# Norms by token parts: latent columns of all features first, the last squares summed by PE, and squares over the outputs between two layers

## What is computed

```python
def rmsnorm(x, g):
    xf = x.astype(jnp.float32)
    y = xf * lax.rsqrt(jnp.mean(xf * xf, axis=-1, keepdims=True) + EPS)
    return (y * g.astype(jnp.float32)).astype(x.dtype)

x = x + gt2 * conv_ffn(modulate(rmsnorm(x, norm2_g[layer]), sh2, sc2), ...)   # first two layers
...
hx = rmsnorm_2(x, g_pre) * (1 + scale[:, None]) + shift[:, None]              # last two layers
x_new = x + gate[:, None] * rmsnorm_2(y, g_post)
```

## Time and profile before

| | |
|---|---|
| runs, median | 2902.92 us (2902.10, 2902.92, 2913.47) |
| profiled execution, own time | 2902.85 us |
| its span | 2901.0 us |
| mean granted clock of PE | 0.946 of full speed |
| PE busy, its instructions | 2635.5 us (91%), 14496 |
| DVE, ACT, POOL busy | 1297.1, 932.1, 173.3 us |
| chain that ended last, by engine | PE 82%, DVE 10%, ACT 4%, DMA 2% |

### The profile page before, as it was taken

The page is one execution under the profiler, slowest core; times in us unless marked ns, Lnnn a source line. Parts: engine busy times, 40 slices in busy tenths (PEclk is TensorE's granted clock), DMA queues, the critical chain, the costliest instruction groups (busy, mean ns, idle before and its releaser), DMA issues.

```text
span 2901.0 us, 35381 instructions
## 1 busy us (share of the span) xinstructions
PE 2635.5 (91%) x14496; PEld 2032.7 (70%) x14496; DVE 1297.1 (45%) x2324; ACT 932.1 (32%) x1619; POOL 173.3 (6%) x134
## 2 busy tenths in 40 slices
PE   4988799997999999989998989999979989949997
PEld 2765555585888888867876667777858866828765
DVE  3235378835333333354435453334452264373463
ACT  3234355623212122234233332222332143332342
POOL 0000001001101011010000010101100001000010
PEclk9999889997999999998999899999979999969898
DMA  5123300011343332211120135553211210102201
GB/s 213 64 70 92 119 13 1 1 44 59 114 132 110 123 118 68 68 55 59 59 73 1 30 121 169 167 171 127 88 55 62 60 54 1 54 23 84 98 1 58
DMA packets 66001, 223.20 MB, mean 77 GB/s; under 512 B 7216, under 2 KB 10928, under 8 KB 65072
## 3 DMA queue, kind: packets, MB, share of 16 engines
q1 hardware_dynamic: 63648, 214.13, 22.9%
q10 hardware_dynamic: 2192, 6.82, 0.6%
HBM read 218.82 MB, written 2.10 MB: 76 GB/s over the span
## 4 chain that ended last, share of the span: by engine, by line
PE 82%; DVE 10%; ACT 4%; DMA 2%; issue 1%; POOL 0%; SPq 0%; DVEq 0%; ACTq 0%
PE pair L959 21%; PE pair L961 20%; PE pair L960 20%; PE pair L1069 4%; DVE T L1790 3%; PE side L934 2%; PE side L1133 2%; PE pair L982 2%; ACT T L1448 2%; PE pair L1120 1%; DMA RAW<-in_w 1%; PE pair L1002 1%; DVE HL L1782 1%; PE pair L653 1%; PE pair L652 1%
## 5 line engine op out<-in xcount | busy, mean ns | idle before, releaser
L959 PE MATMUL pair<-HH,WH 128*128 128x512 f32 (+1 forms) x2432 | 886.5, 365 | 70.2 <-DVE HL L1782 67.5
L961 PE MATMUL pair<-HH,WL 128*128 128x512 f32 (+1 forms) x2432 | 865.6, 356 | 0.0
L960 PE MATMUL pair<-HL,WH 128*128 128x512 f32 (+1 forms) x2432 | 865.3, 356 | 0.0
L959 PEld LDWEIGHTS pair<-HH,WH 128*128 128x128 f32 x2432 | 465.3, 191 | 192.8 <-DVE HL L1782 87.9
L1558 DVE TENSOR_TENSOR WL<-RAW,WH 128x1024 fp32r<-128x1024 f32 (+4 forms) x286 | 320.7, 1121 | 513.0 <-ACT WH L1224 500.4
L961 PEld LDWEIGHTS pair<-HH,WL 128*128 128x128 f32 x2432 | 466.6, 192 | 65.8
L960 PEld LDWEIGHTS pair<-HL,WH 128*128 128x128 f32 x2432 | 467.3, 192 | 62.1 <-issue 2.6
L1224 ACT CAST WH<-RAW 128x1024 fp32r<-128x1024 f32 (+4 forms) x286 | 270.3, 945 | 548.9 <-DMA RAW<-in_w 531.6
L959 PE MATMUL pair<-DH,WH 128*128 128x512 f32 (+3 forms) x624 | 232.8, 373 | 8.4 <-POOL DL L1977 4.3
L960 PE MATMUL pair<-DL,WH 128*128 128x512 f32 (+3 forms) x624 | 223.6, 358 | 0.0
L961 PE MATMUL pair<-DH,WL 128*128 128x512 f32 (+3 forms) x624 | 223.1, 358 | 0.0
(11 more groups left out here) (278 smaller groups left out, 2754.1 us busy)
## 6 DMA issues: line engine op xcount, KB each, us to landing
RAW<-in_w SPq DMA_DIRECT2D x345, 512.0 KB, 3.6
RAW<-in_w SPq DMA_DIRECT2D x49, 384.0 KB, 3.1
RAW<-in_w SPq DMA_DIRECT2D x16, 256.0 KB, 2.7
DFL<-in_dft_lat ACTq DMA_DIRECT2D x4, 1024.0 KB, 7.7
X<-in_x SPq DMA_DIRECT2D x1, 3072.0 KB, 16.4
out_x<-X SPq DMA_DIRECT2D x8, 256.0 KB, 2.0
RAW<-in_w SPq DMA_DIRECT2D x12, 128.0 KB, 2.0
RAW<-in_w SPq DMA_DIRECT2D x8, 144.0 KB, 2.1
```

The source lines that it names most:

```text
L959: mm(out[0:j.m, c:e], wh[k], a, start=k == 0, stop=False)
L960: mm(out[0:j.m, c:e], wh[k], b, start=False, stop=False)
L961: ins = mm(out[0:j.m, c:e], wl[k], a, start=False, stop=k == j.k - 1)
```

## The change

A new `lat_first(t0)` gives the latent range first, then the context. In all six norms and both posts the sums, Ln and Exp, and in the norms the scaling, shift and splitting, are done for the latents of all eight k and then for the context of all eight. The last feature's square is not added by DVE: PE adds T[2] and T[1] with two matmuls that accumulate. Behind a norm with t0 = 0 whose first two jobs also have t0 = 0 (a1, a2, b1, s0), PE computes the latents of both jobs in two pieces of 256 columns and then the context of both. In `yout` the square comes before the copy to YB. Between the two last layers the squares of the new X go to YB, over the outputs that are used up, and PE adds all eight k by itself; of the context DVE adds four k before norm s1's latents and four behind them, and PE sums its squares before the third job. Many waits of an engine on itself are left out. The modulation of `post` moves from AB to PAB. `pe_wait_rhs` waits for the part that a piece needs.

```diff
+def lat_first(t0):
+    return [(0, 0, LAT)] if t0 else [(0, CTX, TOK), (1, 0, CTX)]
...
 # PE
-            for c in range(0, n, 512):
-                e = min(n, c + 512)
+            for c, e in tokens or [(c, min(n, c + 512)) for c in range(0, n, 512)]:
...
+                    elif key[2] == (a < CTX) or (key[2] == 0 and b > CTX):
+                        pe.wait_ge(*step(*key, k))
...
+        def sums_of(s, first, last, key):
+            mm(sum_psum(s), ONES, first, start=True, stop=False)
+            mm(sum_psum(s), ONES, last, start=False, stop=True).then_inc(*pe.mark(*key))
+        def sums_of_columns(s, a, b):
+            for k in range(KD):
+                pe.wait_ge(*step("nsq", "s1", s, k))
+                ins = mm(sum_psum(s), ONES, YB[:, k, a:b], start=k == 0, stop=k == KD - 1)
+            ins.then_inc(*pe.mark("nss", "s1", s))
...
+                held = [j for j in js if j.kind != "ada"][0:2]
+                normed = state["first"] and not any(j.t0 for j in held)
...
+                    if stage == 0 and normed and j is held[0]:
+                        job(j, [(512, TOK), (CTX, 512)], last=False)
+                    elif stage == 0 and normed and j is held[1]:
+                        job(j, [(512, TOK), (CTX, 512)], last=False)
+                        for x in held:
+                            job(x, [(0, CTX)])
+                    elif stage == 0:
+                        if state["columns"] and j not in held:
+                            sums_of_columns(1, 0, CTX)
+                            state["columns"] = False
...
             elif p[0] == "norm":
-                sums(T[2], ONES, n, P, ("nss", q["id"]), ("nacc", q["id"]))
+                if q["id"] == "s1":
+                    sums_of_columns(0, CTX, TOK)
+                    state["columns"] = True
+                else:
+                    pe.wait_ge(*step("nacc", q["id"], KD - 2))
+                    for s, a, b in lat_first(q["t0"]):
+                        pe.wait_ge(*step("nsq", q["id"], s, KD - 1))
+                        sums_of(s, T[2][:, a:b], T[1][:, a:b], ("nss", q["id"], s))
...
 # ACT, yout
-                act.wait_ge(*act.own())
-                A(YB[:, i, 0:n], ps, AF.Copy, scale=1.0).then_inc(*act.mark())
...
-                A(T[i % 2][:, 0:n], ps, AF.Square).then_inc(*act.mark("psum_read", j.n))
+                A(T[i % 2][:, 0:n], ps, AF.Square).then_inc(*act.mark("ysq", j.layer, i))
+                A(YB[:, i, 0:n], ps, AF.Copy, scale=1.0).then_inc(*act.mark("psum_read", j.n))
...
 # ACT, norm
+                if not late:
+                    act.wait_ge(*step("xready", q["id"]))
+                    for s, a, b in lat_first(t0):
+                        root(s, a, b)
+                for s, a, b in lat_first(t0):
+                    if late:
+                        if s:
+                            squares_of_columns(s, a, b)
+                        root(s, a, b)
+                    for k in range(KD):
+                        t = (T[0], T[1], T[4], T[5])[k % 4]
+                        act.wait_ge(*step("nmul", q["id"], s, k))
                         dst = t[:, a:b] if k in POOL_LO else HH[:, k, t0 + a:t0 + b]
-                        act.wait_ge(*act.own())
                         A(dst, t[:, a:b], AF.Identity, bias=modv(q["blk"], q["shift"] + k, s)).then_inc(*act.mark())
...
 # DVE
+        def add_post(l, k, s, a, b):
+            STT(YB[:, k, a:b], YB[:, k, a:b], PAB[:, s, k:k + 1], T[3][:, a:b], ALU.mult, ALU.mult).then_inc(*dve.mark())
+            dve.wait_ge(*dve.own())
+            TT(x, x, YB[:, k, a:b], ALU.add).then_inc(*dve.mark("xfin", l, s, k))
...
+                for s, a, b in lat_first(t0):
+                    if q["id"] == "s1" and s:
+                        for k in range(4, KD):
+                            add_post(0, k, s, a, b)
+                    dve.wait_ge(*step("nrstd", q["id"], s))
+                    for k in range(KD):
...
+                        STT(t[:, a:b], X[:, k, t0 + a:t0 + b], AB[:, s, k:k + 1], T[3][:, a:b], ALU.mult, ALU.mult).then_inc(*dve.mark("nmul", q["id"], s, k))
+                        if k >= 2:
+                            lo(s, a, b, k - 2)
...
 # DVE, post
+                for s, a, b in lat_first(t0):
+                    dve.wait_ge(*step("prstd", l, s))
+                    for k in range(4 if s else KD):
+                        add_post(l, k, s, a, b)
```

More of the change, by code:

```diff
@@ L64, in __init__ @@
         self.sq = None
+        self.pair = None
 def stream(jobs):
@@ L915, in _ @@
         mm = nc.tensor.matmul
-        state = {"hready": [], "first": True}
+        state = {"hready": [], "first": False, "columns": False}
         def take(bank):
@@ L920, in take, with job @@
                 pe.wait_ge(*step(*key))
-        def job(j):
+        def job(j, tokens=None, last=True):
             s = j.n % NRING
@@ L938, in job @@
                 return
-            pr = uses[0] % 2
-            uses[0] += 1
-            take(pr)
-            pe.wait_ge(*step("lo", j.n))
+            if j.pair is None:
+                j.pair = uses[0] % 2
+                uses[0] += 1
+                take(j.pair)
+                pe.wait_ge(*step("lo", j.n))
+            pr = j.pair
             out = pairs[pr]
@@ L1201, in _ @@
                 l = p[1]
-                n = TOK if l == 0 else LAT
-                sums(T[2], ONES, n, P, ("pss", l), ("pacc", l))
-                free[2] = [("prstd", l, "ln")]
+                t0 = 0 if l == 0 else CTX
+                take(2)
+                pe.wait_ge(*step("pacc", l, KD - 2))
+                pe.wait_ge(*step("psq", l))
+                for s, a, b in lat_first(t0):
+                    sums_of(s, T[2][:, a:b], T[1][:, a:b], ("pss", l, s))
+                free[2] = [("prstd", l, s, "ln") for s, a, b in lat_first(t0)]
     @block.scalar
@@ L1345, in square, with squares_of_columns @@
                 act.wait_ge(*step("nacc", q["id"], k - 2))
-            act.wait_ge(*act.own())
-            A(T[k % 2 if k else 2][:, 0:n], X[:, k, q["t0"]:TOK], AF.Square).then_inc(*act.mark("nsq", q["id"], k))
+            if k < KD - 1:
+                if col:
+                    act.wait_ge(*step("xcol", col.n))
+                A(T[k % 2 if k else 2][:, 0:n], X[:, k, q["t0"]:TOK], AF.Square).then_inc(*act.mark("nsq", q["id"], k))
+                return
+            for s, a, b in lat_first(q["t0"]):
+                if col and not (s and col.t0):
+                    act.wait_ge(*step("xcol", col.n, s))
+                A(T[1][:, a:b], X[:, k, q["t0"] + a:q["t0"] + b], AF.Square).then_inc(*act.mark("nsq", q["id"], s, k))
+        def squares_of_columns(s, a, b):
+            for k in range(KD):
+                act.wait_ge(*step("xfin", 0, s, k))
+                A(YB[:, k, a:b], X[:, k, a:b], AF.Square).then_inc(*act.mark("nsq", "s1", s, k))
         def mlsilu(i):
@@ L1362, in _ @@
             act.also("act_end", pi)
-            if p[0] in ("norm", "lownorm", "attn", "mlstm", "post"):
+            if p[0] in ("norm", "lownorm", "attn", "mlstm", "post") and (p[0] != "norm" or p[1]["id"] != "s1"):
                 act.wait_ge(*step("dve_end", pi))
@@ L1387, in _ @@
                             act.wait_ge(ctx_reloaded, 16)
-                        square(q, k)
+                        square(q, k, j if j.kind == "addx" else None)
                     if stage == 1:
@@ L1604, in epilogue @@
                 dve.wait_ge(*step("mm", j.n))
-                for s, a, b in segs(j.t0):
+                for s, a, b in lat_first(j.t0):
                     x = X[:, m["col"], j.t0 + a:j.t0 + b]
-                    dve.wait_ge(*dve.own())
-                    STT(x, pairs[pr][:, a:b], modv(m["blk"], m["gate"] + m["col"], s), x, ALU.mult, ALU.add).then_inc(*dve.mark())
+                    STT(x, pairs[pr][:, a:b], modv(m["blk"], m["gate"] + m["col"], s), x, ALU.mult, ALU.add).then_inc(*dve.mark("xcol", j.n, s))
                 dve.also("psum_read", j.n)
```

131 lines of the change are left out of this document (57 added, 74 removed).

## The result

The changed kernel took 2875.31 us (median of 6 runs, 2871.65 to 2884.08), the kernel before beside it 2901.80 (2891.37 to 2913.47): a ratio of 0.9905, 95% interval 0.9885 to 0.9925. So it is faster by 0.95%, as forecast: 2875 against 2870, inside the range of 2860 to 2884. The profiled execution took 2875.46 (before: 2902.85), 27.4 less.

The account below looks back on a forecast made before the run. DVE's chain of squares, scaling and splitting was taken to bound the norms and post steps, PE everything else. Gains of 4.7+0.8+5.7+1.4+5.7+13+1.3 = 32.6 us from 2902.85 gave 2870, range 2860 to 2884.

Parts of the forecast that it names:

- T0 to the third job: Halved norms, from DVE's start of scaling (T0) to the third job: T0+29.6 against T0+34.7, 5.1 us gained.
- about 4 us: Held jobs after the last latent low half: PE at the low clock at first, 16 pieces at 0.21 us.
- the sign of being wrong: Held jobs of the halved norms: pieces of 0.21 us beyond the first 20 would show the forecast wrong.
- The start of the norm: Ahead of T0: PE's second matmul replaces DVE's last add; net 0.6 us earlier in b1, s0, a2, 0.4 later in a1.
- a2: Norm a2: val 0's late split and gate 1's late load eat nearly all the gain; 0.8 us gained, gate 1 at T0+36.5.
- 27.3, and twice 24 context pieces, 33.1: Norm a2: after val 0's weights at 21.5, 48 pieces end at T0+27.3 and the context pieces at T0+33.1.
- b2: Norm b2, without halves: loses the last add (0.8) and own waits (0.5), gets a second sum; 1.4 us gained.
- I take the high level: Norm b2: two sums at the high clock take 1.97 us; at the low level 0.4 us is lost.
- Between the last layers: Post step and s1: scaling starts 17.5 us earlier, PE idles 9, low clock costs 2.1; 13 us gained.
- The end: Last post phase: copy and add leave the way of the sums, STT overlap; 1.3 us gained.
- rival 1: Norms a1, a2, b1, s0: clock stays low through both held jobs, costing 34 us, time 2904; chance 0.08.
- rival 5: Norms: POOL's subtractions wait for a running DVE instruction, some 1 us a norm, 5 in all, time 2875; chance 0.05.

Follow-up runs that it names:

- run 1: Changed kernel with PE again taking the two held jobs of a1, a2, b1 and s0 in the old order, columns 0 to 511 first: 2886.07 us, ratio 0.9929.
- run 6: Changed kernel with the waits of DVE, ACT and POOL on themselves put back in the norms: 2876.92 us in one run.
- run 9: Changed kernel with the last square of a1, a2, b1, b2 and s0 added by DVE again and one set of ones-matmuls: 2870.23 us in one run.
- run 2: Changed kernel with the first side job of the modulation after val 0 in the first feed-forward stage: 2873.46 us, ratio 0.9889.
- run 5: Changed kernel with no low halves given to POOL, DVE doing all eight of a half: 2859.88 us, ratio 0.9856.
- run 4: Changed kernel with PE's eight context sums in s1 ahead of the second held job: 2873.77 us, ratio 0.9886.
- run 7: Changed kernel with s1's context half behind the splits and epilogues that jobs 3 and 4 need: 2866.52 us, ratio 0.9870.
- run 11: Changed kernel with a2's side jobs after gate 1, plus the edits of run 3, run 7 and run 5: 2840.55 us, ratio 0.9770.
- run 12: Kernel before the change, with no low halves given to POOL and nothing else: 2900.03 us, ratio 0.9981.
- run 3: Changed kernel with b2's last square added by DVE again and one ones-matmul of 512 columns: 2879.53 us in one run.

## Why the prediction was right, and where it was not

- **T0 to the third job** (29.6 forecast; 29.3, 29.7, 29.8 measured) is right, and by its mechanism: run 1 takes PE's order away and gets 33.5 and 34.2. Within it two sizes were off and hardly mattered: the latent half 12.8 to 13.0 for 12.7, the context half 7.7 for 7.1 (its own terms, 6.5 and 0.3, make 6.8). The own waits gave 0.3 to 0.5 in these latent halves, where 0.5 was taken (run 6). The "about 4 us" at the low level stood on no row; it was 3.2, 4.3 and 4.7 us behind the last latent low half in a1, b1 and s0, which makes 14, 19 and 21 pieces of 0.21 (the sign of being wrong was more than 20). In other profiles it was down to 1.5.
- **The start of the norm**: the sum was about right (T0 came 1.0, 1.8 and 0.9 earlier in a2, b1 and s0, for 0.6), but its working put the gain in the wrong term. "PE adds it with a second matmul", 1.03 earlier, gives nothing on the whole; Ln and Exp of the latents alone, ahead of the context, give 1.3 (run 9). In a1 T0 came 0.4 later, as forecast; with one sum it would have come 1.3 earlier.
- **a2**: forecast 0.8 gained, measured 1.3 lost, and 1.6 more in gate 1 at the low level. The mechanism (late split, late load) was named and runs 1 and 2 show it; the failed step is "27.3, and twice 24 context pieces, 33.1" with gate 0's end at 30.2. The held pieces were counted at the high level from the start. PE restarted at 682.32 (T0+22.7, forecast 21.5, which took the context half as done at 19.2, where it took until 20.8), 12 pieces came at 0.21, gate 0 ended at T0+32.8, and the load and split behind it moved by as much.
- **b2**: "I take the high level" failed. The sums ran low after 2.67 us idle, and 0.7 was lost, where the bound of that step said 0.4. Of the runs with two sums there, only run 5's (6.5 us to T0) had the high level throughout.
- **Between the last layers**: DVE's scaling started 17.4 us earlier relative to the last output matmul (forecast 17.5), PE was idle 10.7 (forecast 9), job 3 lost 2.4 to the low clock (2.1). The chain is right in every step, and runs 4 and 7 take it apart; but it gave 11.1 us net, not 13. The context half took 7.7 us, not 6.7, and the written sum is short: 2575.0+3.7+1.0+6.7+1.05+1.23 is 2588.7, not 2588.0.
- **The end**: 1.3, as forecast.
- **The rivals**: rival 1 (clock low through the held jobs) falls: from 2125.4 on, 12.3 us before the third job of s0, the pieces came every 0.12 us. Rival 5 was the strongest of what I held unlikely, and its mechanism is there: POOL and DVE hold each other both ways. The row that I put against it was no evidence. DVE's low half ahead of the subtraction of the earlier trace rows had only 0.14 us left; in run 6, norm b1, 0.66 us were left:

```profile
1694.24 0.75 DVE L1782 SCALAR_TENSOR_TENSOR HL<-T,MOD,HH 128x512 fp32r<-128x512 f32 x1
...
1299.89 0.75 DVE L1855 SCALAR_TENSOR_TENSOR HL<-T,MOD,HH 128x512 fp32r<-128x512 f32 x1
1299.98 1.80 POOL L2014 TENSOR_TENSOR HL<-T,HH 128x512 fp32r<-128x512 f32 x1 [0.74 <-ACT HH L1491]
```

The subtraction of 512 columns took 1.28 us with 0.14 left, 1.75 with 0.63 left (s0, changed kernel) and 1.80 with 0.66 left: what is left of DVE's instruction and 1.12 to 1.14 more each time, and 1.27 to 1.29 where nothing was left. The 1.28 by itself can't tell the two apart, but the subtractions of 768 columns in the kernel before took 2.08 us with 0.40 left and 2.13 with 0.45. So POOL did wait for DVE. The Trainium skill ("SBUF — State Buffer", "SBUF: two separate sides") says of the port pair that the two engines share that it is held for a whole instruction by the one which starts first; these rows agree. But rival 5's price, 1 us a norm on the latent half, didn't come: the latent half was 12.8 us in b1 and s0, where POOL's first subtraction waited 0.63 us, and 13.0 in a1, a2 and b2, where none did. That the time was rival 5's 2875 is chance. What I had missed is the other direction, POOL holding DVE, in work which the change left in place: run 5 prices it at 8 to 11 us in the stages.

The total was right partly by balance. The stages gave 29.2 up to the third jobs, of which the low clock took 4.0 back in s1 and a2: 25.2, where 32.6 were forecast. The start of the program gave 2.8 by chance, and the rest lost 0.6. The POOL hold as the cause of these 8 to 11 us is shown by one constant, twice (runs 5 and 11), and by the groups of DVE; that it was neutral in the kernel before is measured (run 12), and the account of why is worked out from its rows, not tested by itself.

## What to carry to other kernels

When a chain of one engine holds up PE, order PE's own pieces by what arrives first, and check each place for what sits behind in program order on the other engines: three stops of PE in the changed kernel (4.6 and 2.6 us in a2, 10.7 in s1) were weights split or loaded late because of where that stood in an order, not because of its length. Ask of an offload to POOL what DVE's instructions take with and without it. A mean of 1087 ns against 752 for one form is the hint, and the sum over all forms decides: the same offload cost 5.0 us of DVE's time in the changed kernel and 2.4 in the kernel before, where removing it gave nothing clear of the noise. Judge a change of a few us by stage lengths between fixed landmarks, since one stretch at the low clock moves the total by 6, and take more than one profile where the clock level within the stage differs.

## What the hardware showed that I had not expected

- POOL's 512-column subtraction took 1.27 to 1.29 us where no DVE instruction ran at its start, and otherwise what was left of DVE's and 1.12 to 1.14 us: 1.75 when it began 0.12 us after the start of one. A scaling of DVE took 1.09 us on average beside POOL, 0.75 without it.
- Idle time ahead of a stretch doesn't tell PE's clock by itself: sums ran low after 2.67 us idle (b2), high after 3.33 (run 3), and low again after 3.56 (s0). In b1 the idle time was 3.29 us in all eleven profiles with two sums; the first sum ran high in ten of them and low in run 2.
- With no instruction changed, the first window attention stayed at the granted clock of 0.50 for 24 us in one profile and 41 in the other, and its stage took 6 us longer. Over all profiles it was 14 to 41 us.
